# Values of the full-causal heads computed first, with tokens on the partitions, and queries reversed instead of keys

## The reference

```python
h = rms_norm(x, g_mix)
qa, ka, va, qb, kb, vb, ga, gb = split(h @ w_in)      # 512, 512, 512, 512, 128, 128, 1024, 1024 columns
# per head of 64: qa, ka, qb, kb = rms_norm(.) * norm weight
ya = moba_attention(qa, ka, va, bias_a)   # 8 heads; at 512 tokens every past block is selected: full causal
yb = swa_attention(qb, kb, vb, sinks, bias_b)         # 8 query heads, 2 key/value heads, window of 128
merged = sigmoid(ga + b) * (ya @ w_branch_a) + sigmoid(gb + b) * (yb @ w_branch_b)
x = x + merged @ w_out
x = x + square(relu(rms_norm(x, g_ffn) @ w_ff1)) @ w_ff2
```

## Time and profile before

| | |
|---|---|
| median of 3 runs | 678.23 us (677.71 to 678.46) |
| profiled execution | 677.42 us, of which the span from first to last instruction is 675.6 |
| busy: PE, DVE, ACT, POOL | 671.0, 500.7, 369.6, 322.4 us |
| mean granted TensorE clock | 1.000 of full speed |
| chain that ended last | 97% PE |

### The profile page before, as it was taken

How to read it: one execution, slowest core, us unless ns; L and a number is a source line. 1 busy time by engine, 2 the same in 40 slices (tenths; PEclk the granted TensorE clock), 3 DMA queues, 4 the chain that set the end, 5 groups by cost and what they waited for, 6 DMA issues and landing times.

```text
span 675.6 us, 9503 instructions
## 1 busy us (share of the span) xinstructions
PE 671.0 (99%) x3254; PEld 555.3 (82%) x3254; DVE 500.7 (74%) x697; ACT 369.6 (55%) x662; POOL 322.4 (48%) x194
## 2 busy tenths in 40 slices
PE   9999999999999999999999999999999999999998
PEld 7888788888888888888888888888888888888886
DVE  7875898455555555885558879788797888978897
ACT  7765676666665666543348546254463525536360
POOL 0175566455556553444436436246362454435532
PEclk9999999999999999999999999999999999999999
DMA  8223242222322213555222231414133151230303
GB/s 320 94 88 100 69 122 94 80 69 89 108 89 73 69 53 110 156 175 192 85 95 93 96 119 65 155 62 151 66 102 115 62 186 62 93 98 27 125 0 125
DMA packets 22909, 69.87 MB, mean 103 GB/s; under 512 B 2731, under 2 KB 4267, under 8 KB 22876
## 3 DMA queue, kind: packets, MB, share of 16 engines
q1 hardware_dynamic: 22588, 68.92, 30.5%
q10 hardware_dynamic: 288, 0.52, 0.2%
HBM read 67.27 MB, written 2.16 MB: 103 GB/s over the span
## 4 chain that ended last, share of the span: by engine, by line
PE 97%; ACT 1%; DMA 1%; POOL 0%; issue 0%; DVE 0%; SPq 0%
PE bank L1335 22%; PE bank L1337 22%; PE bank L1336 21%; PE bank L1645 8%; PE bank L1644 8%; PE bank L1642 8%; PE bank L1482 2%; PE bank L1495 2%; PE bank L1515 1%; PE bank L1517 1%; DMA store<-x_t 1%; PE bank L1614 1%; PE bank L1361 0%; PE bank L1362 0%; PE bank L1423 0%; POOL w_lo L505 0%
## 5 line engine op out<-in xcount | busy, mean ns | idle before, releaser
L505 POOL TENSOR_TENSOR w_lo<-w_raw,w_hi 128x1024 fp32r<-128x1024 f32 x77 | 190.6, 2480 | 229.1 <-ACT w_hi L594 229.0
L1335 PE MATMUL bank<-x_hi,w_hi 128*128 128x512 f32 x326 | 131.3, 403 | 0.5 <-DVE store L1078 0.4
L1337 PE MATMUL bank<-x_hi,w_lo 128*128 128x512 f32 x326 | 127.5, 391 | 0.0
L1336 PE MATMUL bank<-x_lo,w_hi 128*128 128x512 f32 x326 | 127.0, 390 | 0.0
L1335 PE MATMUL bank<-qk_hi,w_hi 128*128 128x512 f32 x320 | 125.0, 391 | 0.0
L1337 PE MATMUL bank<-qk_hi,w_lo 128*128 128x512 f32 x320 | 124.6, 389 | 0.0
L1336 PE MATMUL bank<-qk_lo,w_hi 128*128 128x512 f32 x320 | 124.5, 389 | 0.0
L594 ACT ACTIVATE w_hi<-w_raw 128x1024 fp32r<-128x1024 f32 x80 | 83.8, 1056 | 57.2 <-PE bank L1337 57.2
L1218 DVE SCALAR_TENSOR_TENSOR store<-bank,softmax,store 128x512 f32<-128x512 f32 x101 | 71.9, 742 | 23.8 <-PE bank L1645 23.8
L1645 PE MATMUL bank<-v_parts,x_lo 128*128 128x512 f32 (+1 forms) x218 | 84.4, 387 | 0.0
L1642 PE MATMUL bank<-v_parts,x_hi 128*128 128x512 f32 (+1 forms) x218 | 84.4, 387 | 0.0
(11 more groups left out here) (167 smaller groups left out, 1177.6 us busy)
## 6 DMA issues: line engine op xcount, KB each, us to landing
w_raw<-slabs SPq DMA_DIRECT2D x80, 512.0 KB, 3.3
bias_m<-slabs SPq DMA_DIRECT2D x16, 512.0 KB, 3.5
qk_hi_again<-slabs SPq DMA_DIRECT2D x16, 512.0 KB, 5.0
store<-x_t SPq DMA_DIRECT2D x16, 256.0 KB, 3.8
bias_m<-tab_dram SPq DMA_DIRECT2D x8, 256.0 KB, 4.2
out<-store SPq DMA_DIRECT2D x7, 256.0 KB, 2.1
bias_m<-tab_dram SPq DMA_DIRECT2D x8, 128.0 KB, 3.6
w_raw<-slabs ACTq DMA_DIRECT2D x1, 384.0 KB, 4.0
```

What stands on the lines that cost most here:

```text
L505: pool.tensor_tensor(w_lo[:, g % WS, :], w_raw[:, g % RAW, :], w_hi[:, g % WS, :].bitcast(F32), ALU.subtract).then_inc(w_lo_ready, 1)
L1335: pe.matmul(out_, wh, xh, start=first, stop=False)
L1336: pe.matmul(out_, wh, xl, start=False, stop=False)
L1337: last = pe.matmul(out_, wl, xh, start=False, stop=end)
```

## The change

The four value slabs of the full-causal heads become the first four slabs (kind "va"), with another layout: slab g holds all 512 value columns for x tiles 2g and 2g+1. A product there has a 128x128 block of x (128 tokens) as the stationary operand and 128x512 of the weights as the moving one, so that tokens come out on the partitions. Four banks stay open over all 8 x tiles, one for each block of 128 tokens; after the last x tile each is scaled by a per-token column (`r_col`) and cut (`va_hi`, `va_lo`). The column comes from four new products of the squares' sums with a column of ones (`mean_squares`), followed by the old row product, both after kt 5. Then come k and q of the window heads, k and q of the others, and the one value slab of the window heads, which is still transposed. The last query slab (16) is summed in the middle of slab 17, and its norm, high part and low part are written in attention, in steps 0, 1 and 2. Queries are held in reversed order instead of keys and values, the bias table is written the other way round, and score groups are (0, 1), (2, 3, 4), (5, 6, 7), (8, 9, 10), (11, 12, 13), (14, 15). SP issues slab 1 ahead of x tile 4.

```diff
-FIRST = 2
+FIRST = 4
-QKV_KIND = ["k", "q", "q", "v", "q", "v", "q", "v"] + ["k", "q"] * 4 + ["v"] * 2
+N_VA = 4
+QKV_KIND = ["va"] * N_VA + ["k", "q", "q", "q", "q"] + ["k", "q"] * 4 + ["v"]
...
+        def ss_bank(n):
+            return bank[3 + n % 2] if n < N_QK - 1 else acc(LAST_Q - 2)
...
+        def va_tile(r):
+            return acc(r)[:, :].rearrange("p (h d) -> p h d", h=2 * N_VA)
...
-        SCORE_GROUPS = [(0, 1, 2), (3, 4, 5), (6, 7, 8), (9, 10, 11), (12, 13), (14, 15)]
+        SCORE_GROUPS = [(0, 1), (2, 3, 4), (5, 6, 7), (8, 9, 10), (11, 12, 13), (14, 15)]
...
@@ SP @@
             for k in range(KT):
+                if k == 4:
+                    load_first(sp, 1)
+                    load_rest(sp, 1)
                 sp.dma_start(store[:, k, :], x_t[k]).then_inc(x_arrived[k], 16)
-            load_first(sp, 1)
-            load_rest(sp, 1)
...
@@ POOL @@
             for step in range(STEPS + 1):
                 if step >= 1:
                     normalise(step - 1)
+                if step == 2:
+                    qk_split_lo(LAST_Q)
...
@@ ScalarE @@
+            def va_hi(r):
+                act.wait_ge(slab_done, N_VA)
+                act.wait_ge(r_col_ready, 2)
+                act.activation(va_hi_part[r], va_tile(r), ACT.Copy,
+                               scale=r_col[:, r:r + 1]).then_inc(va_hi_ready, 1)
...
                 if step == 0:
                     exps(0)
-                    v_hi(N_QKV - 1)
+                    v_hi(LAST_V)
+                if step == 1:
+                    qkv_hi(LAST_Q)
...
@@ VectorE @@
+            def x_mean_squares():
                 dve.wait_ge(ms_done, 1)
+                dve.tensor_scalar(c_inv_sq, bank[4][:, 0:QT], EPS, None, ALU.add).then_inc(ms_ready, 1)
+                dve.wait_ge(ms_done, 2)
                 dve.tensor_scalar(r_inv_sq, bank[5][:, :], EPS, None, ALU.add).then_inc(ms_ready, 1)
+                dve.wait_ge(c_root_ready, 3)
+                refine(r_col, c_root, c_root_sq, c_inv_sq, r_col_ready, 2)
+                dve.wait_ge(r_root_ready, 3)
+                refine(r_all[:, :], r_root, r_root_sq, r_inv_sq, r_ready, 2)
...
+            def va_lo(r):
+                dve.wait_ge(va_hi_ready, r + 1)
+                dve.scalar_tensor_tensor(out=va_lo_part[r], in0=va_tile(r), scalar=r_col[:, r:r + 1],
+                                         in1=va_hi_part[r].bitcast(F32), op0=ALU.mult,
+                                         op1=ALU.subtract).then_inc(va_lo_ready, 1)
...
-                to = pre[n % 2][:, ::-1] if QKV_KIND[g] == "k" else pre[n % 2]
+                to = pre[n % 2][:, ::-1] if QKV_KIND[g] == "q" else pre[n % 2]
...
                     if step == 0 and e == 1:
-                        v_split_lo(N_QKV - 1)
+                        v_split_lo(LAST_V)
+                        qk_norm(LAST_Q)
...
@@ TensorE @@
+            def mean_squares(column, out_):
+                pe.wait_ge(xsum_ready, KT - 1)
+                for r in range(QT):
+                    last = pe.matmul(column[:, r:r + 1], x_sum[:, P * r:P * r + P], ones[:, :],
+                                     start=True, stop=True)
+                last.then_inc(ms_done, 1)
...
+            def va_product(kt, r, n):
+                high, low = va_weight(kt)
...
+                part, moving = ((x_hi, high), (x_hi, low), (x_lo, high))[n]
+                return pe.matmul(acc(r)[:, :], keys_part(part, kt, r), moving, start=(kt == 0 and n == 0),
+                                 stop=(kt == KT - 1 and n == 2))
...
             for kt in range(KT):
+                if kt < 4:
+                    pe.wait_ge(w_hi_ready, kt + 1)
                 else:
+                    pe.wait_ge(w_lo_ready, kt // 2)
+                if kt < 2:
+                    order = [(r, n) for n in range(3) for r in range(QT)]
+                else:
+                    order = [(r, n) for r in range(QT) for n in range(3)]
+                for r, n in order:
+                    last = va_product(kt, r, n)
+                if kt % 2:
+                    last.then_inc(slab_done, 1)
+                if kt == 5:
+                    mean_squares(bank[4], bank[5])
...
+            AFTER = {(g, KT - 1): g - 1 for g in range(N_VA + 1, LAST_V)}
+            AFTER[LAST_V, 4] = LAST_Q
...
-            qkv_read(N_QKV - 2)
             for step in range(STEPS):
                 if step == 2:
                     pe.wait_ge(pre_ready, N_QK)
                     pe.wait_ge(pre_v_ready, N_V)
                     pe.wait_ge(v_lo_ready, N_V)
+                    pe.wait_ge(va_lo_ready, QT)
```

## The result

The changed kernel takes 679.44 us (median of 22 runs, 677.50 to 681.08); the kernel before took 678.18 in 22 runs beside it. The forecast was 678.9.

The account below looks back on a forecast made before the run. TensorE, busy 671.0 of 675.6 us, bounds the kernel. Terms -0.5 + 0.9 - 1.8 + 0.55 + 1.8 - 0.3 = +0.65 on a median of 678.23 gave 678.9 us; range 676.5 to 680.9.

Parts of the forecast that it names:

- the forecast's own case: Whole kernel: gains and new waits about cancel, 678.9 us, own range 677.7 to 680.1, chance 0.5.
- Start: First 72 products: each x tile feeds 12 products, so PE waits less for x; -0.5 us, bounds 0 and 1.05.
- Slab 3's low part: Before kt 6: DVE's low part of slab 3 comes in time, margin 1.4 us, so no wait.
- rival D: Start: slab 1 ahead of x tiles 4 to 7 delays DVE's chain by over 1.4 us; +1.3, 680.2, chance 0.08.
- Column products: After kt 5: four added one-column products, two load-and-multiply pairs each, cost 0.9 us, bounds 0.44 and 2.1.
- Slab 17: After kt 4 of slab 17: PE waits 0.55 us for the low part of slab 16's squares, slowed beside POOL.
- Step 2: Attention step 2: PE idles 2.35 us behind slab 16's norm and the step 1 maxima; net +1.8, bounds 0 and 2.8.
- Step 8 and slab 20: Attention: the old wait for POOL's w_lo at step 8 goes, -0.3 us; slab 20's w_lo stays hidden, margin 1.0.
- Rival B: Attention step 2: the wait is covered, ScalarE and DVE coming 2.35 us sooner; 676.5 us, chance 0.2.
- Rival C: Attention: the delay passes on through w_lo of slab 20, PE waits about another 1.3 us; 680.2, chance 0.17.
- Rival E: After the 2.35 us idle in attention, PE goes on at its lower clock; +3, 681.9 us, chance 0.05.
- The 0.8 us added for the median: Whole kernel: the old profiled execution lay 0.8 us below its median, so the sum was added to the median.

Follow-up runs that it names:

- the swap: Changed kernel with slab 16's norm ahead of the value copy's low part (v_split_lo) on DVE: 677.08 us, ratio 0.9986.
- the later head sum: Changed kernel with the head sum of slab 16 one x tile later in slab 17, after kt 5: 678.84 us, ratio 1.0005.
- the old kernel with a delay: Kernel before the change with four extra unread DVE passes behind v_split_lo of attention step 0: 679.95 us, ratio 1.0035.
- with the start: Changed kernel with slab 16's norm ahead of v_split_lo, and the first two squares and their sum ahead of slab 2's cuts: 676.46 us, ratio 0.9976.
- the deferred norm: Changed kernel with slab 16's root, norm and copies later in attention, its head sum after kt 5, seven score groups: 677.29 us, ratio 0.9988.

## Why the prediction was right, and where it was not

**Outcome.** 679.44 lies in the range and in the likeliest class, 0.5 over the forecast. But the forecast's own case, gains and waits that cancel, holds for the runs without the fall (-0.3); the median is that plus a rival that had a chance of 0.05. That it lies only 0.5 from the forecast is in part luck: the sum left out the fall, 1.5, and was 0.3 too low besides, while the step from the profiled execution to the median was 1.3 too high.

**Start, forecast -0.5, measured -0.95.** The step that failed: "about 0.5 of that are the first gaps, which PE has right after its warm-up and will have again". PE's first 72 products lose 16.46 - 16.36 = 0.1. The old kernel's three traces agree from the twelfth product on (9.35 to 9.39), whenever its first came, so its first gaps never set the end: they lay inside the time in which it waited for x tiles to arrive and be cut.

**Slab 3's low part, forecast covered, measured 0.30 + 0.47.** The step that failed: "DVE has the same work ahead of it as before (only the cuts of slabs 0 and 1 move)". The diff also moves slab 2's cuts ahead of the squares. ScalarE stood idle 1.10 us for slab 2's transfer and DVE 1.48 for ScalarE, where they used to take squares and sums, so the chain ended 1.84 later (23.29 against 21.45), more than the margin of 1.4. From the cut of slab 2 to slab 3's low part it is 9.10 where it was 7.48 (21.45 - 13.97): 1.62 of the 1.84 is the order, the rest the later cut. Putting half of that back (0.8, by the table on the start) gave 0.74. It is rival D's place, at 0.8 instead of 1.3, and mainly by the order on the engines; but the new order also lets the transfer of slab 2 set the end, and what slab 1's new place in the queue does to that transfer no run shows. With 0.77 for both waits this trace has the most of the six with this start; the others have 0 to 0.5.

**Column products, forecast 0.9, measured 0.81 to 0.91.** Right, by the transposes' 0.11 for each pair. **Transposes, -1.8:** one group is left in the value slab.

**Slab 17, forecast 0.55, measured 0.56**, by the wait and the instruction named: L993 takes 2.03 beside POOL's copy. Moving the sum gave only 0.4 to 0.5 of it back, since the gate product then waits 0.3.

**Step 2, forecast 2.35, measured 2.37.** T is 114.46. DVE takes up the value copy at T + 5.65 (forecast 5.7), and the maxima end at T + 9.3 (9.4). **Step 8 and slab 20, forecast -0.3 and hidden:** both so.

**Rival B** would have needed DVE 2.35 us sooner; the swap shows that 1.0 is to be had and what stops the rest. **Rival C** did not come.

**Rival E, chance 0.05, price 3.** It came in 16 of 22 runs, at 1.54 in the trace and 1.6 to 1.8 between the groups of runs of this kernel and of the later head sum, 2.4 in the old kernel with a delay. The step that failed: its chance was put low since no gap of before was long enough to show it, which is no evidence against it; beside the experiments the kernel before has a clock of 0.997 in 3 of its 79 runs. The price was put high by reading the start's 0.57 gap as the cost of every product. The clock granted there, from 5.5 to 8.0, is 1.00, so that gap was not the clock's; at the lower clock the products of 512 columns follow at 0.43, 0.2 over pace. The Trainium skill, "TensorE: Matmul & The Clock Gate", Part 1, says that what watches the engine's activity runs free and does not reset when the kernel starts, and that the transition point varies by that. Two groups of runs of one kernel, and falls 0.7 and 1.6 us after the stop in its two traces, agree with it; no run here shows the mechanism.

**The 0.8 us added for the median.** The terms without the fall sum to +1.0 on the profiled execution, 678.4, while the runs without it have a median of 677.9. With the 0.8 added, they would have been forecast at 679.2, 1.3 too high. The offset of 0.8 belongs to the old kernel; for the swap it is 0.3 (span 675.0 profiled, 675.3 median) and with the start 0.0. So the step that failed is carrying it over. Of the 0.5 that is left even without it, 0.3 is the traced execution's own, late at kt 6: it took 679.88 where the runs with the fall have a median of 679.6. The rest, and why the old kernel's offset is 0.8, stay open.

## What to carry to other kernels

When a change lets PE stop in mid-run, price the stop twice: its length, and what follows it at the lower clock, here 1.5 us, in two of three executions for stops of 2.4 us and none in 32 for 1.4, with 4 in 112 where PE hardly stopped. Look for two groups in the run times and the mean clock before explaining a median, and fill or shorten the stop: from 2.4 to 1.4 was enough here, to 2.2 was not. When a diff lists what it moves at an engine's head, follow that engine's whole queue to the one wait that matters; an unmentioned reordering behind a transfer cost 0.8 here, most of what the start had gained. And before a difference of under 1 us between two variants is explained, compare their traces from a point that both pass in the same state: a start that depends on a transfer hid the 0.5 that the deferred norm had gained.

## What the runs showed of the hardware

The granted clock fell to half after stops of 1.95 to 2.4 us with PE busy before and after, not at once but some time after the work had gone on: 0.7 us in the changed kernel's first trace (the scores from 123.93 to 124.60 still follow at 0.11 to 0.17), 1.6 in its second, 1.2 in the old kernel with a delay. It fell in part of the executions only. Extra products in the stop, read by nobody, made the kernel 1.4 to 1.6 us faster. A full-precision product with one moving column costs two load-and-multiply records and 0.2 us. Elementwise passes over SBUF on DVE and POOL at the same time lengthen each other: 0.69 to 1.67 on DVE and 1.29 to 1.80 on POOL; the DVE pass that was under way when POOL's was issued kept its 0.69.
